# Feed-forward chunks 1 to 5 computed feature by feature, with the high and low halves of the input side by side as one 512-column operand

## The reference, cut to what matters

```python
f = rms_norm(h, ln_pre_ffn[i])
f = (jax.nn.silu(f @ w_ffn_gate[i]) * (f @ w_ffn_up[i])) @ w_ffn_down[i]
h = h + rms_norm(f, ln_post_ffn[i])
...
hf = rmsnorm(x, g_ffn_pre)
ff = (jax.nn.silu(hf @ w_gate) * (hf @ w_up)) @ w_down
x = x + rmsnorm(ff, g_ffn_post)
```

## Time and profile before

| | |
|---|---|
| median of three runs | 962.51 us |
| lowest and highest | 962.43, 964.66 us |
| the profiled execution | 962.74 us, with a span of 960.9 us and 1.8 us around it |
| mean granted TensorE clock | 0.998 |
| feed-forward chunks 1 to 5 of block 1 | 381.3 to 484.4 us of the span |
| feed-forward chunks 1 to 5 of block 2 | 790.7 to 893.8 us of the span |

### The profile page before, as it was taken

One profiled execution on the slowest core, in us unless ns is written; L12 is line 12 of the kernel. 1 busy time (PEld: TensorE's weight loads), 2 busy tenths in 40 slices (PEclk: granted clock), 3 DMA queues, 4 the chain that ended last, 5 costly groups with the idle time before them and its releaser, 6 DMA issues.

```text
span 960.9 us, 14619 instructions
## 1 busy us (share of the span) xinstructions
PE 951.2 (99%) x5676; PEld 810.6 (84%) x5676; DVE 364.1 (38%) x859; ACT 498.4 (52%) x727; POOL 742.9 (77%) x593
## 2 busy tenths in 40 slices
PE   9999999999999999999999999999999999999997
PEld 8988879988788888888888887899888888888885
DVE  4775627685536234121123245062332341111103
ACT  5493634465544456545454566585566464444431
POOL 5888645875746988899787987878876889888890
PEclk9999999999999999999999999999999999999999
DMA  7645342554435766777554665645564567666531
GB/s 262 213 148 188 111 131 88 180 165 139 142 101 160 244 218 178 228 215 202 177 170 151 204 222 171 232 153 181 172 211 138 161 177 213 194 178 195 175 131 44
DMA packets 76750, 167.33 MB, mean 174 GB/s; under 512 B 8349, under 2 KB 13705, under 8 KB 76553
## 3 DMA queue, kind: packets, MB, share of 16 engines
q1 hardware_dynamic: 71296, 156.40, 52.5%
q10 hardware_dynamic: 5384, 9.99, 3.1%
HBM read 165.32 MB, written 1.05 MB: 173 GB/s over the span
## 4 chain that ended last, share of the span: by engine, by line
PE 96%; DVE 2%; ACT 0%; DMA 0%; issue 0%; DVEq 0%; ACTq 0%
PE L L514 23%; PE L L516 22%; PE L L515 22%; PE Q L516 2%; PE Q L514 2%; PE Q L515 2%; PE L L887 1%; PE L L888 1%; PE L L889 1%; PE Q L731 1%; PE Q L1186 1%; PE L L785 1%; PE L L787 1%; PE L L786 1%; PE Q L849 1%; PE L L824 1%
## 5 line engine op out<-in xcount | busy, mean ns | idle before, releaser
L501 POOL TENSOR_TENSOR w_lo<-raw,w_hi 128x512 fp32r<-128x512 f32 x588 | 741.5, 1299 | 194.4 <-ACT w_hi L1334 194.0
L1334 ACT CAST w_hi<-raw 128x1024 fp32r<-128x1024 f32 x294 | 305.2, 1054 | 261.5 <-PE L L516 122.8
L514 PE MATMUL L<-w_hi,uH 128*128 128x512 f32 (+1 forms) x768 | 304.2, 396 | 0.3
L516 PE MATMUL L<-w_hi,uL 128*128 128x512 f32 (+1 forms) x768 | 296.4, 386 | 0.0
L515 PE MATMUL L<-w_lo,uH 128*128 128x512 f32 (+1 forms) x768 | 295.9, 385 | 0.0
L516 PEld LDWEIGHTS L<-w_hi,uL 128*128 128x128 f32 x768 | 144.3, 188 | 29.7
L514 PEld LDWEIGHTS L<-w_hi,uH 128*128 128x128 f32 x768 | 144.4, 188 | 29.1 <-DVE uL L1935 1.5
L515 PEld LDWEIGHTS L<-w_lo,uH 128*128 128x128 f32 x768 | 144.6, 188 | 26.1
L514 PE MATMUL L<-w_hi,hH 128*128 128x512 f32 x176 | 69.0, 392 | 0.0
L516 PE MATMUL L<-w_hi,hL 128*128 128x512 f32 x176 | 68.6, 390 | 0.0
L515 PE MATMUL L<-w_lo,hH 128*128 128x512 f32 x176 | 68.5, 389 | 0.0
(11 more groups left out here) (363 smaller groups left out, 1285.5 us busy)
## 6 DMA issues: line engine op xcount, KB each, us to landing
raw<-in_w_in SPq DMA_DIRECT2D x88, 512.0 KB, 3.6
raw<-in_w_ffn_gate SPq DMA_DIRECT2D x22, 512.0 KB, 3.7
raw<-in_w_ffn_up SPq DMA_DIRECT2D x22, 512.0 KB, 3.6
raw<-in_w_ffn_down SPq DMA_DIRECT2D x22, 512.0 KB, 3.5
raw<-in_w_gate SPq DMA_DIRECT2D x22, 512.0 KB, 3.7
raw<-in_w_up SPq DMA_DIRECT2D x22, 512.0 KB, 3.6
raw<-in_w_down SPq DMA_DIRECT2D x22, 512.0 KB, 3.5
raw<-in_w_out SPq DMA_DIRECT2D x16, 512.0 KB, 3.6
```

What stands on the lines that cost most here:

```text
L501: last = nc.gpsimd.tensor_tensor(lo[:, cc], raw[:, n % RAW, cc], hi[:, cc].bitcast(F32), ALU.subtract)
L514: mm(dst, sH, wH, start=start, stop=False)
L516: return mm(dst, sL, wH, start=False, stop=stop)
L1334: copy(halves[SLOT[u]][0], raw[:, u % RAW, :]).then_inc(w_hi_there, 1)
```

## The change

In chunks 1 to 5 the roles are exchanged. The stationary operand is a 128 x 128 piece of the weight; what streams is the input. `uH` and `uL` become two halves of one tensor `uu`, so that wH meets both in one matmul of 512 columns (256 of uH, 256 of uL), and wL meets uH in one of 256 columns, added to the first half. There are two matmuls for each k and each feature tile, in place of three of 512 columns for each k and each token tile. The result has features on the partitions, so nothing of these chunks is turned. A bank now holds two parts (0:256 and 256:512) that have to be added, and the factor of a token now lies along the free axis: two matmuls in chunk 0 spread `rstd_h` over the partitions, VectorE copies that to `row_h`. For each feature tile of gate and up ScalarE copies the second part to `small_part`, VectorE adds it and multiplies by `row_h`. Gates are in Q[0..3], ups in L[0..3] (Q[2..3] in chunk 5). Chunk 0 stays in token layout; it is turned in the down step, at k = 1, and the down product takes the features in the order 4 to 21, 0 to 3.

```diff
-ROW_ORDER = {("out2",): (4, 5, 6, 7, 0, 1, 2, 3)}
+ROW_ORDER = {("out2",): (4, 5, 6, 7, 0, 1, 2, 3),
+             ("down", 1): (*range(4, FF // P), 0, 1, 2, 3),
+             ("down", 2): (*range(4, FF // P), 0, 1, 2, 3)}
...
-        uH = place("uH", [P, KD, SEQ], F32R)
-        uL = place("uL", [P, KD, SEQ], F32R)
+        uu = place("uu", [P, 2, KD, SEQ], F32R)
+        uH, uL = uu[:, 0], uu[:, 1]
...
@@ skewed_columns (TensorE, chunk 0)
+                    if j == 3 and first[0][0] == "ffn":
+                        for t in range(NT):
+                            pe.wait_ge(*VE(source, "rstd", t))
+                            last = mm(Q[0][:, t * P:(t + 1) * P], rstd_h[:, t:t + 1].to_broadcast([P, P]), ident, start=True, stop=True)
@@ TensorE, chunks 1 to 5
-                    for j in range(half):
-                        column_unit(step, j, [Q[0], Q[1]] if c == 1 else [L[0], L[2]], n)
-                    if c > 0:
...
-                                    last = turn(Q[2 * (c % 2) + j][:, i * SEQ + t * P:i * SEQ + (t + 1) * P],
-                                                hm[:, t, (2 * j + i) * P:(2 * j + i + 1) * P], ident)
...
-                    for j in range(half, 2 * half):
-                        column_unit(step, j, [L[1], L[3]] if c < 5 else [Q[1], Q[0]], n)
+                    for j in range(2 * half):
+                        n0 = NUMBER[step, j]
+                        pe.wait_ge(w_lo_there, n0 + 1)
+                        wH, wL = unit(n0, per)
+                        banks = gates if j < half else ups(c)
+                        for i in range(per):
+                            k = (j % half) * per + i
+                            for f in range(n // P):
+                                if k == 0:
+                                    if j == 0 and c == 1:
+                                        pe.wait_ge(*VE(prev, "row"))
+                                    elif j == 0:
+                                        pe.wait_ge(*AC(prev, "silu", f))
+                                    elif c == 1:
+                                        pe.wait_ge(*VE(prev, "hidden", 1))
+                                    elif c == 5:
+                                        pe.wait_ge(*AC(prev, "silu", 2 + f))
+                                    else:
+                                        pe.wait_ge(*VE(prev, "lo", f))
+                                feature = slice(f * P, (f + 1) * P)
+                                if k < KD - 1:
+                                    mm(banks[f][:].rearrange("p (a n) -> p a n", a=2), wH[:, i, feature], uu[:, :, k, :], start=k == 0, stop=False)
+                                    last = mm(banks[f][:, 0:SEQ], wL[:, i, feature], uH[:, k, :], start=False, stop=False)
...
+                        last.then_inc(w_used, 1)
@@ TensorE, down
+                        if k == 1:
+                            pe.wait_ge(*AC(("ffn", blk, 5), "silu", 1))
...
+                                    last = turn(Q[j][:, i * SEQ + t * P:i * SEQ + (t + 1) * P],
+                                                hm[:, t, (2 * j + i) * P:(2 * j + i + 1) * P], ident)
...
+                        elif k == 4 and blk == 1:
+                            pe.wait_ge(*VE(prev, "lo", 1))
+                            pe.wait_ge(*VE(("ffn", blk, 5), "lo", 1))
@@ ScalarE
+            def up_parts(step, count):
+                act.wait_ge(*fed(step))
+                for f in range(count):
+                    copy(small_part[:, f, :], ups(step[2])[f][:, SEQ:]).then_inc(*AC.mark(step, "up part", f))
+            def hidden_high(step, f):
+                act.wait_ge(*VE(step, "hidden", f))
+                copy(hH[:, 4 * step[2] + f, :], ups(step[2])[f][:, 0:SEQ]).then_inc(*AC.mark(step, "hi", f))
@@ ScalarE, chunk c > 0
+                    if c > 1:
+                        up_parts(("ffn", blk, c - 1), 4)
+                    for f in range(4 if c > 1 else 0):
+                        hidden_high(("ffn", blk, c - 1), f)
+                        if f < half:
+                            split_up_to(FREED[FIRST[step] + f] - (f == half - 1))
                     split_up_to(FREED[FIRST[step] + half - 1] - 1)
                     act.wait_ge(*fed(step, half))
+                    for f in range(n // P):
+                        copy(small_part[:, f, :], gates[f][:, SEQ:]).then_inc(*AC.mark(step, "gate part", f))
+                    for f in range(n // P):
+                        act.wait_ge(*VE(step, "gate", f))
+                        actf(hidden_part(f), gates[f][:, 0:SEQ], ACT.Silu).then_inc(*AC.mark(step, "silu", f))
+                        if f == 1:
+                            split_up_to(FREED[FIRST[step] + half])
+                    if (blk, c) == (1, 1):
+                        act.wait_ge(landed["mem"], 16)
+                        for t in range(NT):
+                            actf(xv[:, t, :], mem[:, t, :], ACT.Square, accum_out=ss[:, 4 + t:5 + t]).then_inc(*AC.mark(("mem",), "ss", t))
...
                     split_up_to(FREED[consumed - 1] - 1)
@@ VectorE
+            def summed(bank, f, *name):
+                tt(bank[:, 0:SEQ], bank[:, 0:SEQ], small_part[:, f, :], ALU.add)
+                tt(bank[:, 0:SEQ], bank[:, 0:SEQ], row_h, ALU.mult, *name)
+            def hidden_out(step, count):
+                banks = ups(step[2])
+                def low(f):
+                    dve.wait_ge(*AC(step, "hi", f))
+                    k = 4 * step[2] + f
+                    tt(hL[:, k, :], banks[f][:, 0:SEQ], hH[:, k, :].bitcast(F32), ALU.subtract, step, "lo", f)
+                for f in range(count):
+                    dve.wait_ge(*AC(step, "up part", f))
+                    summed(banks[f], f)
+                    dve.wait_ge(*AC(step, "silu", f))
+                    tt(banks[f][:, 0:SEQ], banks[f][:, 0:SEQ], hidden_part(f), ALU.mult, step, "hidden", f)
+                    if f:
+                        low(f - 1)
+                low(count - 1)
@@ VectorE, chunk c > 0
+                    if c > 1:
+                        hidden_out(("ffn", blk, c - 1), 4)
                     if (blk, c) == (1, 2):
                         for t in range(NT):
                             dve.wait_ge(*AC(("mem",), "ss", t))
                             ts(rv[:, t:t + 1], ss[:, 4 + t:5 + t], 1.0 / D, EPS, ALU.mult, ALU.add)
                             rsqrt_one(rstd_m[:, t:t + 1], rv[:, t:t + 1], ("mem",), "rstd", t)
...
+                    for f in range(n // P):
+                        dve.wait_ge(*AC(step, "gate part", f))
+                        summed(gates[f], f, step, "gate", f)
```

More of the change, by code:

```diff
@@ L376, in tiny @@
             free[0] += n
[L377 removed]
+            assert free[0] <= 960 + SEQ
             return small[:, free[0] - n:free[0]]
@@ L418, in build @@
         r1, floor = tiny(8), tiny(8)
+        row_h = tiny(SEQ)
         baH = big("baH", 36, [P, KD, 16], F32R)
@@ L1189, in _ @@
-                    for j in range(half, 2 * half):
-                        column_unit(step, j, [L[1], L[3]] if c < 5 else [Q[1], Q[0]], n)
+                    prev = ("ffn", blk, c - 1)
+                    per = UNIT // n
+                    for j in range(2 * half):
[21 more added lines that the diff above has]
+                                    last = mm(banks[f][:, 0:SEQ], wL[:, i, feature], uH[:, k, :], start=False, stop=False)
+                                else:
+                                    mm(banks[f][:, 0:SEQ], wL[:, i, feature], uH[:, k, :], start=False, stop=False)
+                                    last = mm(banks[f][:].rearrange("p (a n) -> p a n", a=2), wH[:, i, feature], uu[:, :, k, :], start=False, stop=True)
+                        last.then_inc(w_used, 1)
@@ L1651, in _ @@
                 elif kind == "down":
-                    prev = ("ffn", step[1], 5)
+                    blk = step[1]
+                    up_parts(("ffn", blk, 5), 2)
+                    for f in range(2):
+                        hidden_high(("ffn", blk, 5), f)
+                    split_up_to(FREED[FIRST[step] - 1])
+                    for j in range(2):
+                        prev = ("ffn", blk, 0)
+                        act.wait_ge(*PE(prev, "turned", j))
+                        copy(hH[:, 2 * j:2 * j + 2, :], Q[j][:].rearrange("p (k n) -> p k n", k=2)).then_inc(*AC.mark(prev, "hi", j))
                     if step[1] == 1:
@@ L1723, in _ @@
                     half = (LAST[step] + 1 - FIRST[step]) // 2
+                    if c == 0:
+                        split_up_to(FREED[FIRST[step] + half - 1] - 1)
+                        act.wait_ge(*fed(step, half))
+                        act.wait_ge(*VE(("next", "mix" if blk == 1 else "x"), "rstd", 1))
+                        for t in range(NT):
+                            actf(sil[:, t, :], L[2 * t][:], ACT.Silu, scale=rstd_h[:, t:t + 1]).then_inc(*AC.mark(step, "silu", t))
+                        split_freed(step, 2 * half - 2)
```

(34 more changed lines are left out.)

69 lines of the change are left out of this document (29 added, 40 removed).

## The result

| | before | after |
|---|---|---|
| median | 962.84 us | 965.38 us |
| lowest to highest | 962.43 to 964.70 | 962.20 to 968.14 |
| ratio, 95% interval | | 1.0021 [1.0014, 1.0028] |
| the profiled execution | 962.74 us, span 960.9 | 965.03 us, span 963.2 |

The account below looks back on a forecast made before the run. TensorE was taken to bound the kernel, never waiting in the chunks examined. Its terms gave -4.9 us, the wait in chunk 2 of block 1 +2.4, together -2.5: median 962.51 to 960.0 us, range 957.3 to 963.5.

Parts of the forecast that it names:

- 576 pairs: Chunks 1 to 4, both blocks: a 512- and a 256-column matmul take 227 + 120 = 347 ns, nothing on top.
- `row_h` matmuls: Chunk 0: two matmuls in each block, four in all at 0.13 us, +0.5 us; their wait for rstd covered.
- wait in chunk 2 of block 1: TensorE waits for bank L[3], freed late by a copy behind a cast awaiting a DMA: 2.3 us, +2.4 in all.
- the second stretch: Wide matmul's input read as two stretches of 256 columns: possible extra start of 13 ns, taken as zero.
- the sign of a wrong sum: New matmuls in the trace: anything above 351 ns a pair would show the sum on TensorE wrong.
- the break-even: Pairs: from 4.3 ns on top of 347 the change loses; each ns costs 0.58 us over 576 pairs.
- The rival: Pair dearer than 347 ns through a start for the second stretch; 966.2 us at the full 13 ns; chance 0.12.
- The issue gap: Skill page's 131 ns for 512 columns and 81 for 128 would make the change lose; set aside for the trace.
- The turns: Turns on TensorE fall from 88 to 16, 72 x 0.109 us, -7.8 us; their wait for chunk 5's silu covered.
- No wait: Rival: no wait in chunk 2 of block 1, so the gain stays -4.9 us, 957.6 us; chance 0.22.
- The ring in chunks 3 and 4: Rival: raw buffers stay the limit there too, three waits of up to 2.3 us; 961.5 to 964.5 us; chance 0.10.
- VectorE slows GpSimd: Rival: a GpSimd unit exceeds 2.78 us and sets the pace of eight chunks; 970 us and above; chance 0.03.

Follow-up runs that it names:

- grouped_order2: order2_start with the four wide matmuls of each k ahead of the four narrow ones; 960.78 us, ratio 0.9967 to the kernel before.
- all_wide: order2_start with the 256-column matmul of each pair made a 512-column one too, adding the low-by-low product; 1019.53 us, one execution.
- adjacent: The changed kernel with the high and low half of each k side by side in uu, one stretch of 512 columns; 963.46 us, ratio 1.0002.
- grouped: The changed kernel without casts between hH copies, GpSimd's first subtraction held back, and each k's matmuls grouped by width; 962.17 us, ratio 0.9989.
- order2_start: The changed kernel with GpSimd's first subtraction held back and ScalarE's casts one unit later; 961.69 us, ratio 0.9982; second batch 962.03 us, ratio 0.9984.
- start_before: The kernel before, with GpSimd's first subtraction waiting until VectorE has done its two scalings of x; 962.73 us, ratio 0.9997.
- start_after: The changed kernel, with GpSimd's first subtraction waiting until VectorE has done its two scalings of x; 963.63 us, ratio 1.0004.
- order: The changed kernel with ScalarE's four copies to hH of a chunk first and the casts behind them; 962.78 us, ratio 0.9991.
- again: The changed kernel once more, unaltered, against the kernel before; 964.40 us, ratio 1.0009.

## Why the prediction was wrong, point by point

The profiled execution went from 962.74 to 965.03, +2.3 us, where the sum said -2.5. The 4.8 us between them ("measured" from the profiles of before and after):

| step | predicted | measured | difference |
|---|---|---|---|
| start of the program | 0 | +1.9 | +1.9 |
| 576 pairs | 347 ns | 352.5 ns | +3.2 |
| `row_h` matmuls | +0.5 | +1.0 | +0.5 |
| input waited for in chunk 0 of block 2 | 0 | +0.4 | +0.4 |
| wait in chunk 2 of block 1 | +2.4 | +1.1 | -1.3 |

They add up to +4.7; 0.1 us stays unassigned. This accounts for the two profiled executions; the medians are 2.5 us apart.

- *What bounds the kernel.* Right. TensorE's own sequence sets the time, and in the repaired kernels every nanosecond of a pair counts in full: 2.2 ns less in grouped_order2 make 1.3 us over 576 pairs, and the median fell by 0.9 to 1.25 us.
- *The pair.* This is the step that cost most. I put nothing on top of 227 + 120, "because both lengths fit the same 'columns plus 13 ns' whichever operand stands still". Both rows were of unmixed streams, and all_wide shows that the wide one is right for those. That a sequence of two lengths costs their sum was the unshown part. I had named it, and then put the possible cost on the second stretch, which adjacent showed to be free. The pair measured 352.5 ns, above the 351 that I had set as the sign of a wrong sum; the break-even, 4.3 ns, stood in the text, and the measured 5.5 lie above it: with the wait, the change loses by this term alone. The rival was given 0.12, the right mechanism (a dearer pair) with a wrong reason. A row of the kernel before could have warned me, where the 256-column matmuls of chunk 5 end and 512-column ones follow:

```profile
484.26 0.28 PE L516 MATMUL Q<-w_hi,uL 128*128 128x256 f32 x1
484.38 0.40 PE L514 MATMUL L<-w_hi,hH 128*128 128x512 f32 x1
...
485.54 0.39 PE L516 MATMUL L<-w_hi,hL 128*128 128x512 f32 x1
485.77 0.39 PE L514 MATMUL L<-w_hi,hH 128*128 128x512 f32 x1
```

The first five wide ones take 485.54 - 484.38 = 1.16 us, 232 ns each; only then it is 227.

- *The issue gap.* The kernels show 227 ns for 512 columns and 117 to 120 ns for 256. The 131 and 81 ns for 512 and 128 columns of the Trainium skill, page "TensorE: Matmul & The Clock Gate", section "Back-to-back issue gap", do not hold for these operands, as 227 ns in the earlier trace rows already said.
- *The turns and `row_h`* stand thus in after's groups by form (against the earlier trace rows):

```profile
L1234 PE MATMUL Q<-table,hm 128*128 128x128 f32 x16 | 2.1, 272 | 0.0
...
L695 PE MATMUL Q<-table,small 128*128 128x128 f32 x8 | 1.2, 274 | 0.0
```

- *The turns.* Right in after: 16 are left, 72 fewer, and their wait for chunk 5's silu is covered, though not in grouped (1.0 us). From chunk 1 to the down product a block takes 101.52 us in order2_start and 103.05 in start_before, 1.5 less. By the terms it is 40 turns (-4.4), the matmuls (+1.25) and the excess of 288 pairs (+1.6): also -1.5.
- *`row_h`.* Mis-sized: eight matmuls in all (x8 above), not four. In block 1 they put 0.36 us between their neighbours, and the wide matmuls right behind them are 0.1 us slower in all: from the last matmul ahead of them to chunk 1 it is 3.43 us where it was 2.95, so 0.48 for a block instead of 0.25. The cover for their wait held.
- *The input in chunk 0 of block 2.* A term that I had put at nothing. VectorE begins the low half of `uu` 0.45 us behind ScalarE's cast, where it was 0.10 before, and TensorE waits for it. Why is open.
- *The wait in chunk 2.* Right in place, chain and sign, including the cast behind f = 2 and the copy behind it. Its length, 1.1 us, came from TensorE being late, by 1.9 us from the start alone; with the start repaired it is 2.1 us, 0.2 off my 2.3. What I had not priced is the clock behind it. A late start and a wait share one slack, so that in the changed kernel repairing the first made the second longer: this is why single remedies (start_after, order) left it level with the kernel before and both together did not.
- *Rivals.* No wait: excluded by the trace. The ring in chunks 3 and 4: no wait there. VectorE slows GpSimd: not in the chunks, where GpSimd's 26 instructions take 32.63 us (1.255 each); but at the start GpSimd held up VectorE, the same pair of engines with the roles changed. I had used only one of the two conditions of the page that I cited, two SBUF inputs.

```profile
426.59 32.63 POOL L515 TENSOR_TENSOR w_lo<-raw,w_hi 128x512 fp32r<-128x512 f32 x26 [2.88 <-ACT w_hi L1370]
```

- *The start.* No step of mine looked at it, since the change does not touch it. No row of mine lies there, though the kernel before showed the near miss: VectorE's scalings begin 0.30 us ahead of GpSimd, the second one 0.03 us. The rise of the clock comes at another time in each execution: 7.2 us in after (both scalings held up), 6.5 in again (one), 5.4 in order and 4.7 in adjacent (none), whose first 13 us are the same program. Whether the change makes it later on the whole stays open.
- *The upper runs of after*, to 968.1 us, may have another cause than the start. Of its 20 executions 12 have a mean granted clock of 0.997 or less, all of them at 965.17 us or more; so have the four of start_after above 965 us, among them the one whose profile shows the clock falling behind the wait (0.997). The profiled one of after, with the late rise, has 0.998. Of the 61 executions of the kernels without the wait in chunk 2 (order, grouped and all with both remedies) none has so low a clock, of 84 later ones of the kernel before six have. That fits a fall behind the wait in most executions of after, and then the wait costs more than the 1.1 us of its profile; only a profile would show it.

## What to carry to other kernels

A price read from a stream of equal instructions holds for such a stream; where a change mixes two lengths, set the break-even per instruction first, and if it is a few nanoseconds, the forecast is open, however well the rows fit. Do not put an instruction that may wait for a transfer ahead of one that frees a bank for the bounding engine: made one unit later, the same casts cost nothing here. And look in the kernel before for near misses between engines, 0.3 us here, since any change can turn them, and even a second run.

## What the runs showed of the hardware

- A 512-column matmul takes 226.7 ns among its like (all_wide), 236 on average between 256-column ones (117 ns each; after) or about 230 in the cheap rhythm (adjacent), 232 in groups of four (119; grouped).
- At half clock a pair takes 640 ns, which is 768 columns at 1.2 GHz with nothing on top; at full clock 33 ns come on top of 320. No fixed cost shows at the low clock.
- A wait of 1.95 us was followed by 3.4 us at half clock (start_after). The Trainium skill, page "TensorE: Matmul & The Clock Gate", section "What's actually happening", has two levels and nothing between, and the trace agrees: 1.00 and 0.50 only.
- Two VectorE scalings of 128x256 with input and output in SBUF take 0.62 us, or 2.58 us if a GpSimd subtraction starts 0.1 us earlier.
